# The opening block of a three-block transformer kernel: sum of squares moved from VectorE to GpSimd, x loaded whole, order of the first steps changed

## The reference, cut to what matters

```python
def _rmsnorm(x, g):
    xf = x.astype(jnp.float32)
    y = xf * lax.rsqrt(jnp.mean(xf * xf, -1, keepdims=True) + EPS) * g.astype(jnp.float32)
    return y.astype(x.dtype)
...
        h = _rmsnorm(x, norm_mix[layer])
...
            p = h @ ev_w_in[j]
```

## Time and profile before

| | us |
|---|---|
| median of 3 runs (lowest, highest) | 3628.23 (3622.12, 3631.38) |
| the profiled execution | 3628.23 |
| its span, first to last instruction | 3626.4 |
| TensorE busy in the span | 3333.6 (92%) |
| VectorE busy | 2040.0 (56%) |
| ScalarE busy | 940.6 (26%) |
| GpSimd busy | 462.1 (13%) |

### The profile page before, as it was taken

How to read it: one execution, slowest core, us unless ns; L and a number is a source line. 1 busy time by engine, 2 the same in 40 slices (tenths; PEclk the granted TensorE clock), 3 DMA queues, 4 the chain that set the end, 5 groups by cost and what they waited for, 6 DMA issues and landing times. The chain is left out here.

```text
span 3626.4 us, 50871 instructions
## 1 busy us (share of the span) xinstructions
PE 3333.6 (92%) x21218; PEld 2721.2 (75%) x21218; DVE 2040.0 (56%) x2756; ACT 940.6 (26%) x1662; POOL 462.1 (13%) x363
## 2 busy tenths in 40 slices
PE   7889999999899999899969889899989779899998
PEld 6678788878778877688748777687868568688786
DVE  6455644444464454699856663434446565688744
ACT  2036300111342241223253440222020460100104
POOL 0000111000013552100024430000020000100001
PEclk9899999999999999999989999999999889999998
DMA  3111122232304553332200003222222202322221
GB/s 131 50 54 48 47 93 93 79 108 90 87 28 159 186 174 112 103 110 94 73 28 4 3 4 116 70 93 93 93 71 93 96 1 82 104 93 93 73 96 70
DMA packets 210403, 298.62 MB, mean 82 GB/s; under 512 B 32802, under 2 KB 111278, under 8 KB 210062
## 3 DMA queue, kind: packets, MB, share of 16 engines
q1 hardware_dynamic: 210190, 295.59, 24.4%
HBM read 291.25 MB, written 4.32 MB: 82 GB/s over the span
## 5 line engine op out<-in xcount | busy, mean ns | idle before, releaser
L447 PE MATMUL bank<-h_hi_cut,ring_hi_cut 128*128 128x512 f32 x1960 | 774.9, 395 | 60.8 <-DVE h_cut L538 15.9
L447 PE MATMUL bank<-h_hi_cut,ring_cut 128*128 128x512 f32 x1960 | 768.2, 392 | 0.0
L447 PE MATMUL bank<-h_cut,ring_hi_cut 128*128 128x512 f32 x1864 | 731.5, 392 | 0.0
L500 DVE CAST ring_hi_cut<-ring 128x4096 fp32r<-128x4096 f32 (+3 forms) x97 | 197.7, 2038 | 641.0 <-DMA ring<-in_ffn_w_gu 138.6
L447 PEld LDWEIGHTS bank<-h_hi_cut,ring_hi_cut 128*128 128x128 f32 x1960 | 371.1, 189 | 145.9 <-issue 42.9
L447 PEld LDWEIGHTS bank<-h_hi_cut,ring_cut 128*128 128x128 f32 x1960 | 370.7, 189 | 79.9
L447 PEld LDWEIGHTS bank<-h_cut,ring_hi_cut 128*128 128x128 f32 x1864 | 353.0, 189 | 76.0 <-issue 2.2
L502 DVE TENSOR_TENSOR ring_cut<-ring,ring_hi_cut 128x4096 fp32r<-128x4096 f32 (+3 forms) x97 | 380.6, 3923 | 7.6 <-issue 0.4
L447 PE MATMUL bank<-hidden_cut,ring_hi_cut 128*128 128x512 f32 x848 | 324.9, 395 | 0.0
L447 PEld LDWEIGHTS bank<-hidden_cut,ring_hi_cut 128*128 128x128 f32 x848 | 159.9, 189 | 40.1 <-issue 1.2
L332 POOL TENSOR_TENSOR work<-work 128x512 f32<-128x512 f32 x35 | 52.7, 1507 | 1003.6 <-ACT work L316 1003.4
(11 more groups left out here) (606 smaller groups left out, 5909.1 us busy)
## 6 DMA issues: line engine op xcount, KB each, us to landing
ring<-in_ffn_w_gu SPq DMA_DIRECT2D x44, 1024.0 KB, 6.5
ring<-in_w_in SPq DMA_DIRECT2D x21, 2048.0 KB, 7.8
ada_w<-in_ada_w SPq DMA_DIRECT2D x12, 2048.0 KB, 8.0
ring<-in_w_up SPq DMA_DIRECT2D x22, 1024.0 KB, 6.8
ring<-in_w_ff_in SPq DMA_DIRECT2D x8, 2048.0 KB, 8.6
ring<-in_w_ff_out SPq DMA_DIRECT2D x8, 2048.0 KB, 8.0
ring<-in_ffn_w_down SPq DMA_DIRECT2D x8, 1536.0 KB, 6.6
ring<-in_w_out SPq DMA_DIRECT2D x6, 2048.0 KB, 7.9
```

The source lines that it names most:

```text
L447: last = nc.tensor.matmul(to, lhs, rhs, start=st and q == 0, stop=sp_ and q == len(parts) - 1)
L500: dve.tensor_copy(high, whole)
```

## The change

Six things differ, all in the opening block but the last two:

- x is loaded by one transfer into `h`, ahead of `squares`, instead of two halves into `c_qkv` behind it.
- The six small tables are issued by ScalarE on its own queue, at its start, instead of by SyncE.
- TensorE makes the four bias products first (banks 4 to 7) and then turns x; VectorE likewise adds the masks first. VectorE copies all eight banks before the first h_cut, since h_cut lies where x was loaded.
- ScalarE rounds slab 0 before the Squares. GpSimd adds the squares, seven additions with a drain behind each, inside the block.
- In the first projection VectorE's reduction is gone, and the sums on TensorE stand behind the second tile without a wait for it.
- The parameter `add_squares` of `project` goes.

```diff
             def taker(eng, taking, j, i=None, at_two=None):
@@ -561,8 +559,6 @@
                 cut_tiles(dve, 0)
                 cut_slab(dve, 1)
                 cut_tiles(dve, 1)
-                if add_squares:
...
-            if add_squares:
-                tail_sum.advance(1)
...
+            xtok = h[:].rearrange("p k s -> p (k s)").rearrange("p (t d) -> p t d", t=ST)
...
+            sq = [c_hi_f[:, k, :] for k in range(DT)]
...
-                    half_x = [slice(0, D // 2), slice(D // 2, D)]
-                    x_of = lambda part: a["x"][:, part].rearrange("(t p) d -> p t d", p=P)
-                    for dst, src in ((squares[:], a["c_squares"][:, 0:NTOP * P].rearrange("p (n q) -> p n q", n=NTOP)),
-                                     (xtok[:, :, half_x[0]], x_of(half_x[0]))):
+                    for dst, src in ((xtok, a["x"].rearrange("(t p) d -> p t d", p=P)),
+                                     (squares[:], a["c_squares"][:, 0:NTOP * P].rearrange("p (n q) -> p n q", n=NTOP))):
                         sp.dma_start(dst, src).then_inc(loaded.sem, 16)
                     sp.dma_start(vecs[:], a["vecs"]).then_inc(vecs_here.sem, 16)
-                    sp.dma_start(xtok[:, :, half_x[1]], x_of(half_x[1])).then_inc(mx["back"].sem, 16)
-                    for dst, src in ((table[:, 0:8], a["t5_bias"]), (table[:, 8:12], a["rel_bias_3"]),
-                                     (onehot[:, 0, :], a["c_onehot_a"]), (onehot[:, 1, :], a["c_onehot_d"]),
-                                     (mask8[:, 0, :], a["c_logtimes"]), (mask8[:, 1, :], a["c_causal_d"])):
-                        sp.dma_start(dst, src).then_inc(padded.sem, 16)
...
                 def _(pe):
+                    pe.wait_ge(padded.sem, padded.done(5))
+                    for n, (c0, heads) in enumerate(((0, 8), (0, 8), (8, 4), (8, 4))):
+                        nc.tensor.matmul(bank[4 + n][0:heads, :], table[:, c0:c0 + heads], onehot[:, n // 2, n % 2 * S:n % 2 * S + S],
+                                         start=True, stop=True).then_inc(turned.sem, 1)
                     pe.wait_ge(loaded.sem, loaded.done(1))
                     for k in range(DT):
-                        if k == 4:
-                            pe.wait_ge(mx["back"].sem, mx["back"].done(0))
+                        if k >= 4:
+                            pe.wait_ge(dve_half.sem, dve_half.done(k - 4))
                         for t in range(ST):
                             last = nc.tensor.transpose(bank[k][:, t * P:(t + 1) * P], xtok[:, t, k * P:(k + 1) * P], ident)
                         last.then_inc(turned.sem, 1)
-                    pe.wait_ge(padded.sem, padded.done(5))
-                    for n, (c0, heads) in enumerate(((0, 8), (0, 8), (8, 4), (8, 4))):
-                        pe.wait_ge(dve_took.sem, dve_took.done(n))
-                        nc.tensor.matmul(bank[n][0:heads, :], table[:, c0:c0 + heads], onehot[:, n // 2, n % 2 * S:n % 2 * S + S],
-                                         start=True, stop=True).then_inc(turned.sem, 1)
...
                 def _(dve):
+                    dve.wait_ge(padded.sem, padded.done(5))
+                    for n, heads in enumerate((8, 8, 4, 4)):
+                        dve.wait_ge(turned.sem, turned.done(n))
+                        cols = slice(n % 2 * S, n % 2 * S + S)
+                        dve.tensor_tensor(toep[0:heads, n // 2, cols], bank[4 + n][0:heads, :], mask8[0:heads, n // 2, cols],
+                                          ALU.add).then_inc(dve_half.sem, 1)
+                    for k in range(DT):
+                        dve.wait_ge(turned.sem, turned.done(4 + k))
+                        dve.tensor_copy(x[:, k, :], bank[k][:]).then_inc(dve_took.sem, 1)
                     dve.wait_ge(vecs_here.sem, vecs_here.done(0))
+                    dve.drain()
                     for k in range(DT):
-                        dve.wait_ge(turned.sem, turned.done(k))
-                        dve.tensor_copy(x[:, k, :], bank[k][:]).then_inc(dve_took.sem, 1)
-                        if k >= 2:
-                            tail_on_dve(dve, k - 2, gain0)
-                    for k in (DT - 2, DT - 1):
                         tail_on_dve(dve, k, gain0)
-                    for n, heads in enumerate((8, 8, 4, 4)):
-                        dve.wait_ge(turned.sem, turned.done(DT + n))
-                        cols = slice(n % 2 * S, n % 2 * S + S)
-                        dve.tensor_tensor(toep[0:heads, n // 2, cols], bank[n][0:heads, :], mask8[0:heads, n // 2, cols],
-                                          ALU.add).then_inc(dve_half.sem, 1)
...
                 @block.scalar
                 def _(act):
+                    for dst, src in ((table[:, 0:8], a["t5_bias"]), (table[:, 8:12], a["rel_bias_3"]),
+                                     (onehot[:, 0, :], a["c_onehot_a"]), (onehot[:, 1, :], a["c_onehot_d"]),
+                                     (mask8[:, 0, :], a["c_logtimes"]), (mask8[:, 1, :], a["c_causal_d"])):
+                        act.dma_start(dst, src).then_inc(padded.sem, 16)
                     act.wait_ge(vecs_here.sem, vecs_here.done(0))
                     for k in range(DT):
                         act.wait_ge(dve_took.sem, dve_took.done(k))
                         act.activation(h_hi[:, k, :], x[:, k, :], ACT.Copy, scale=gain0(k)).then_inc(tail_hi.sem, 1)
-                    for k in range(DT):
-                        act.activation(c_hi_f[:, k, :], x[:, k, :], ACT.Square)
                     act.wait_ge(weights_here[0].sem, weights_here[0].done(g_ev_in["dmas"] - 1))
                     for part in halves:
                         act.activation(ring_hi[:, 0, part], ring[:, 0, part], ACT.Copy).then_inc(early_hi.sem, 1)
+                    for k in range(DT):
+                        act.activation(sq[k], x[:, k, :], ACT.Square).then_inc(tail_sq.sem, 1)
 
...
                     pool.memset(rpb, 0.0).then_inc(consts_made.sem, 1)
+                    for k in range(1, DT):
+                        pool.wait_ge(tail_sq.sem, tail_sq.done(k))
+                        pool.tensor_tensor(sqsum, sqsum if k > 1 else sq[0], sq[k], ALU.add)
+                        pool.drain().then_inc(tail_sum.sem, 1)
...
-                def sum_squares(dve):
-                    dve.tensor_reduce(sqsum, c_hi_f[:].rearrange("p k s -> p s k"), AX, ALU.add)
-                    dve.drain().then_inc(tail_sum.sem, 1)
```

More of the change, by code:

```diff
@@ L359, in project @@
                     act_tail=None, pool_tail=None, join=None, both=None, dve_first=None, dve_second=None, slab_pre=None, pe_tail=None, dve_tail=None,
-                    sp_end=None, k_order=None, add_squares=None):
+                    sp_end=None, k_order=None):
             split = hi is not None
@@ L449, in pe_slab @@
                     last.then_inc(tile_done.sem, 1)
-                    if rms and i is None and j == 0 and m == (2 if add_squares else 1):
-                        if add_squares:
-                            pe.wait_ge(tail_sum.sem, tail_sum.done(0))
+                    if rms and i is None and j == 0 and m == 1:
                         sums_on_pe(pe, join is not None)
@@ L2811, in build @@
                         mode=lambda j: "tok" if j in (5, 8) else "ch", cols=lambda j: 64 if j == 4 else 512, sp_body=table_here, pe_body=c_on_pe,
-                        pe_wait=roots_read, act_body=c_on_act, dve_body=c_on_dve, pool_body=c_on_pool, slab_pre=swapped_columns, add_squares=sum_squares)
+                        pe_wait=roots_read, act_body=c_on_act, dve_body=c_on_dve, pool_body=c_on_pool, slab_pre=swapped_columns)
                 rows_stored.advance(1)
```

5 lines of the change are left out of this document (1 added, 4 removed).

## The result

The changed kernel takes **3646.04 us** (median of six runs, 3641.3 to 3650.8; the fifteen on record have 3646.40), the kernel before beside it 3627.4 (six runs, 3622.12 to 3631.38). The ratio is 1.0053, with a 95% interval of 1.0043 to 1.0064: 18.6 us slower. Forecast were +8.7 us and 3636.9, with a range up to 3642.6. The direction and the place were right, but the forecast was less than half of what came.

A forecast was written before the change was run, and what follows sets the result against it. The prediction took the start of TensorE's first projection, set by the opening block's end, as what counts: GpSimd's additions move it from 29.74 to near 38.4, the first projection adds nothing, so 3628.23 + 8.7 = 3636.9 us, range 3629 to 3642.6.

The forecast's parts named there:

- What bounds the kernel: Whole kernel: TensorE is busy 92% of the span, so the change counts as a shift of the projection's start, then 29.74.
- The start of the transposes: Opening block, TensorE: first transpose at 12.0 us, waiting for x, with the table matmuls (3.60 us) hidden by that wait.
- ScalarE: Opening block: Copies from 15.3 to 20.2 us, rounding to 23.9, Squares last, the second one ending at 25.0.
- VectorE: Opening block: copies end at 18.6 us, h_cut at 24.0, ring_cut at 28.5 if unheld; held by GpSimd, at 29.7.
- GpSimd: Opening block's new last engine: seven additions, the first held to 27.4 us, the last ending at 38.2; projection start +8.7.
- The rival without blocking: Opening block: GpSimd's additions run unblocked beside VectorE, ending at 35.3 us; start +5.9, time 3634.1; chance 0.10.
- The first projection: Removing VectorE's 7.50 us reduction and moving the sums costs nothing, bounds −1 to +0.5 us; the slow first 5.7 us simply move.
- The rival with the reduction on the path: First projection: VectorE's reduction did hold TensorE, so removing it gains 7.5 us, giving 3629.4; chance 0.06.
- The rival of the late x: Opening block loads: x's 4096-byte rows move slowly, 5.7 us more, 3642.6; decided by transposes starting from 14.2 on; chance 0.17.
- a sign of an error: Whole span: the forecast is wrong if the difference at the span's end isn't that at the start of the projection.

The follow-up runs named there:

- The two delays: Kernel before with 31 or 25 idle additions on GpSimd in the opening block, each with a drain: 3642.5 and 3636.2 us.
- a_turn_first: Changed kernel with TensorE's transposes ahead of the bias products again and VectorE's mask additions last: 3641.45 us, ratio 1.0043.
- a_reduction: Changed kernel with the sum of squares back on VectorE in the first projection and no additions on GpSimd: 3636.08 us, ratio 1.0026.
- b_pool_sum: Kernel before with slab 0 rounded ahead of the Squares and the squares added on GpSimd inside the opening block: 3633.64 us, ratio 1.0019.
- b_round_first: Kernel before with only ScalarE's rounding of slab 0 moved ahead of its eight Squares: 3624.72 us, ratio 0.9996.
- a_warm: Changed kernel with six extra products on a zeroed tile on TensorE ahead of the bias products: 3648.39 us, ratio 1.0058.
- a_tab_sp: Changed kernel with the six table loads back on SyncE's queue behind vecs: 3644.95 us, ratio 1.0047.
- b_act_pad: Kernel before with twelve drains at the start of ScalarE's part of the opening block, no load moved: 3629.98 us, ratio 1.0007.
- a_both: Changed kernel with transposes ahead of the bias products, masks last, and the sum of squares back on VectorE: 3634.83 us, ratio 1.0019.
- a_both_sp: Changed kernel with transposes first, masks last, the reduction on VectorE, and the tables back on SyncE behind vecs: 3628.29 us, ratio 1.0002.
- b_one_act: Kernel before with a single table load of 1 KB (t5_bias) on ScalarE's queue: 3627.23 us, ratio 0.9997.
- b_again: Kernel before, unchanged, with a second profile of its own: 3626.58 us, ratio 0.9995.
- b_delay31: Kernel before with 31 idle additions on GpSimd in the opening block, a drain behind each: 3642.5 us, ratio 1.0043.

## Why the prediction was wrong

**What bounds the kernel: right.** All turns on the start of the projection. The two delays show one for one, and in the changed kernel the start's 16.8 us are nine tenths of the 18.6.

**The start of the transposes: this step failed.** It holds 7.8 of the 9.9 us by which the forecast of the loss was short (8.1 at the start of the projection, 1.8 behind it). The prediction put the transposes at 12.0, with the sentence that the tables "should be here by 8, so that these matmuls end by about 11.6 and are hidden by the wait for x". Measured: 19.76. Three things were wrong in it. The tables landed at 12.84, not by 8; on a queue of their own they still moved beside x, squares and vecs, at 293 GB/s for all together from 6 to 10 us, and the forecast had counted just these bytes ahead of the transposes (2625 KB, 12.6 us), but not ahead of the tables. The eight products took 6.99 and not 3.60 us, because in the trace of before they stand behind 32 transposes, and here they come first on a cold TensorE. And the cover was counted the wrong way: once the tables are last to land, all of the products stand in series ahead of the transposes. The text had said that without that cover the start would be "later by a few tenths"; the wait for the tables and the products were worth 7.8 us. For the bytes alone the 12.0 was good: 12.30 in a_turn_first. (The 12.6 itself is a slip: 52 KB fewer than in front of the second half are worth 0.1 to 0.3 us at 396 or 201 GB/s, so 12.4 to 12.5.)

**ScalarE: right,** counted from the first transpose. First Copy +3.2 (forecast 3.3), rounding +8.1 (8.2), second Square done about +13.0 (13.0).

**VectorE: right,** +12.1 for the end of h_cut (12.0), +16.6 for the end of ring_cut (16.5, if nothing holds it). Nothing held it; the forecast had it held for 1.1.

**GpSimd: the sum right, the path in part.** From the first transpose to the start of the projection it is 26.74 against a forecast of 26.4. The first addition was blocked as forecast, but not by one subtraction: it stood through both, and ended 1.1 us behind the second (37.44). The forecast had let it in between the two, delaying the second; its second addition ended 18.8 behind the first transpose, the measured one 19.1. That the sum agrees is in part luck: one error of +2.3 us (the first addition's end) met one of −2.0 (the second addition wasn't held too). The pitch then was 1.44, not 1.48. By single edits the additions cost 9.9 (a_reduction) and 9.5 us (b_pool_sum against b_round_first), where the forecast implies 38.4 − 28.8 = 9.6. The Trainium skill, "SBUF — State Buffer", section "SBUF: two separate sides", has the later one block fully; the 4.73 and 3.87 us agree, and so do 4.61, 5.31 and 5.37 us in a_turn_first, a_warm and a_tab_sp, each ending 1.1 behind VectorE's pair. The rival without blocking is refuted. In all five the addition became ready while a subtraction was running.

**The first projection: the sums and the reduction at nothing, right.** With the reduction back (a_reduction) no stop appears on TensorE, and the stops of 6.4 and 9.2 us stayed. The rival with the reduction on the path is refuted, and with it the gain of 7.5 us that the prediction had set beside it. One detail was wrong: the slow first products did not "simply move". The half clock lasts 5.8 us from the start in before and 3.8 in the changed kernel (until 50.3), so 0.9 us came back within 10 us.

**The rival of the late x: refuted as put.** It had the length of x's rows as its reason and 14.2 as its threshold. The transposes are later than that, but x wasn't: together with the squares behind it, it was complete by 12.30, and by 10.06 without the tables beside it.

**The last 1.8 us, and why the end isn't the start.** The prediction named this as a sign of an error, and it is one. In six kernels whose tables are all on ScalarE's queue the time beyond the start is +1.8 to +7.0 us, in eight others −0.7 to +0.4, and in b_act_pad +3.2. The same edit does it in a_both against a_both_sp: 6.5 us in the medians, 2.4 at the start. In the profiles it is no single loss. If the products of TensorE are matched one by one, the changed kernel is behind before by 16.8 us at the start, 15.9 at 100 us, 11.4 at 500, 15.0 at 2860 and 18.2 at the end; most of these steps, of both signs, go with a longer or shorter stretch at half the clock, and over the whole span the two profiles hold the same amount of it (295.6 and 295.7 us). The one step that tells the groups apart is 2860 to 2901 us of before, far from the change: it is there in five of those six (+2.8 to +3.1 us) and in none of the other nine, b_act_pad included (at most 0.3). It was picked out afterwards among several. Here are the same products, first in before, then in after (the columns are those of the earlier trace rows):

```profile
2890.00:2895.00 5.00, 4.01 (x11) 2.19 (x12) 3.04 (x7) 2.39 (x5) 3.79 (x8) 1.00 0.00 0
```

```profile
2905.10:2910.10 5.00, 4.06 (x9) 2.08 (x8) 2.54 (x6) 0.80 (x2) 3.04 (x6) 0.50 0.00 0
```

TensorE has the granted clock of 2.4 GHz in the one and of 1.2 GHz in the other, at the same point of the program and after nearly the same pauses. What in the opening block decides this 2800 us later stays open, and so does the cause of the 1.8 us; a single load on the queue doesn't do it (b_one_act), and part of such shifts is chance, as b_again shows.

## What to carry to other kernels

A piece of work is hidden behind a wait only if its own input is there before the other's: for a step that is moved to the front, work out the landing of its own data by all bytes issued beside it, whatever the queue, and give it the duration that its engine shows at its first work (here 0.87 us a product, not 0.45). Where a block ends with a meeting of all engines, a sum that was in slack inside the next block (7.5 us on VectorE, nothing on the path) is paid for as soon as it is moved in front of that meeting onto an engine that then arrives last (9.9 us on GpSimd). The same goes for small things put last, as the mask additions and the stores behind them. Then read the shift at the start and at the end of the trace apart: the first is the change, the second holds several us of both signs that mostly go with the clock and that a second profile of the same kernel doesn't repeat.

## What the runs showed of the hardware that wasn't expected

- A clock of 1.00 at the start of these profiles is no measurement. The trace of the changed kernel has its first entry for the clock at 23.0 us, and the views show 1.00 ahead of it; between 16 and 20 us the bias products take 0.87 us each, against 0.45 in before. In a_warm the first entry is at 7.8 us, and there the distance between the added products falls from 0.85 to 0.43 us. The rate of the products is the better witness.
- A GpSimd addition that becomes ready while VectorE runs the first of two subtractions with two SBUF inputs, the second queued directly behind, waits for both: 4.73 and 3.87 us instead of 1.26, and VectorE loses nothing (4.49 and 4.47 us for the pair, as in the earlier trace rows). Where GpSimd's additions are already running, VectorE loses: in b_delay31 the pair took 5.44 us and an h_cut 0.92 instead of 0.74, and at 1472 us of before a single subtraction lost 0.93.
- Small tables on a second queue are not free. They lower the rate from 414 to 293 GB/s while x is coming, and delay vecs from 8.8 us (a_tab_sp) to 11.8.
